# Unsummed weights for the sample's cached values: two key chunks on the column halves of TensorE, row blocks added afterwards

## The reference, cut to what matters

```
s = einsum('bqhcd,bkhcd->bhcqk', q, k) * (DIFF_HD ** -0.5)   # c: the two softmaxes
p = softmax(s, axis=-1)
a = p[:, :, 0] - lam * p[:, :, 1]
return einsum('bhqk,bkhe->bqhe', a, v)                       # v: 512 cached rows + 32 new ones
```

## Time and profile before

| | |
|---|---|
| median of 3 runs | 2252.79 us (2252.65 to 2253.14) |
| the profiled execution | 2255.4 us, its span 2253.5 us |
| PE busy | 2216.9 us, 98% of the span |
| DVE busy | 1196.4 us, 53% |
| ACT busy | 973.8 us, 43% |
| POOL busy | 856.4 us, 38% |
| mean granted clock of TensorE | 0.997 |

### The profile page before, as it was taken

The page is one execution under the profiler, slowest core; times in us unless marked ns, Lnnn a source line. Parts: engine busy times, 40 slices in busy tenths (PEclk is TensorE's granted clock), DMA queues, the critical chain, the costliest instruction groups (busy, mean ns, idle before and its releaser), DMA issues.

```text
span 2253.5 us, 43144 instructions
## 1 busy us (share of the span) xinstructions
PE 2216.9 (98%) x17640; PEld 2091.3 (93%) x17640; DVE 1196.4 (53%) x2018; ACT 973.8 (43%) x1876; POOL 856.4 (38%) x378
## 2 busy tenths in 40 slices
PE   6999999999999999999999999999999999999998
PEld 6889888889999999999988889888899999999998
DVE  5676665545456563256255666644463556523553
ACT  5555554344323453244345555533352334523443
POOL 4244223234343433443443343232243434434433
PEclk9999999999999999999999999999999999999999
DMA  4232222222222222322322232222222222223222
GB/s 164 68 109 76 91 68 94 73 82 80 75 76 94 76 88 79 107 82 71 103 89 72 86 104 81 75 82 73 82 78 78 76 94 81 77 86 105 94 65 98
DMA packets 81651, 193.69 MB, mean 86 GB/s; under 512 B 7504, under 2 KB 36528, under 8 KB 81456
## 3 DMA queue, kind: packets, MB, share of 16 engines
q1 hardware_dynamic: 59696, 173.50, 23.3%
q10 hardware_dynamic: 21760, 17.45, 2.4%
HBM read 177.50 MB, written 13.42 MB: 85 GB/s over the span
## 4 chain that ended last, share of the span: by engine, by line
PE 95%; ACT 2%; DVE 2%; issue 1%; POOL 0%; DMA 0%; ACTq 0%; DVEq 0%; POOLq 0%
PE ps L619 14%; PE ps L621 14%; PE ps L620 14%; PE ps L670 7%; PE ps L671 6%; PE ps L672 6%; PE ps L1023 4%; PE ps L1024 4%; PE ps L1022 4%; PE ps L693 2%; PE ps L771 2%; PE ps L803 2%; PE ps L838 2%; PE ps L649 2%; PE ps L896 2%; PE ps L763 1%
## 5 line engine op out<-in xcount | busy, mean ns | idle before, releaser
L497 POOL TENSOR_TENSOR wlo<-raw,whi 128x1024 fp32r<-128x1024 f32 (+1 forms) x330 | 768.0, 2347 | 1056.4 <-ACT whi L1081 1056.4
L619 PE MATMUL ps<-hl,whi 128*128 128x272 f32 x2432 | 704.0, 289 | 0.0
L621 PE MATMUL ps<-hl,wlo 128*128 128x272 f32 x2432 | 701.2, 288 | 0.0
L620 PE MATMUL ps<-hl,whi 128*128 128x272 f32 x2432 | 700.0, 288 | 0.0
L619 PEld LDWEIGHTS ps<-hl,whi 128*128 128x128 f32 x2432 | 458.6, 189 | 1.5
L621 PEld LDWEIGHTS ps<-hl,wlo 128*128 128x128 f32 x2432 | 457.6, 188 | 0.0
L620 PEld LDWEIGHTS ps<-hl,whi 128*128 128x128 f32 x2432 | 457.0, 188 | 0.0
L1081 ACT ACTIVATE whi<-raw 128x1024 fp32r<-128x1024 f32 (+1 forms) x330 | 313.4, 998 | 203.0 <-PE ps L1024 176.6
L670 PE MATMUL ps<-whi,hl 128*128 128x256 f32 x1216 | 353.1, 290 | 4.6 <-ACT rawk L1176 4.3
L671 PE MATMUL ps<-wlo,hl 128*128 128x256 f32 x1216 | 344.6, 283 | 0.0
L672 PE MATMUL ps<-whi,hl 128*128 128x256 f32 x1216 | 344.1, 283 | 0.0
(11 more groups left out here) (223 smaller groups left out, 3286.1 us busy)
## 6 DMA issues: line engine op xcount, KB each, us to landing
raw<-in_w_units_dram SPq DMA_DIRECT2D x260, 512.0 KB, 4.6
raw<-in_w_down_units_dram SPq DMA_DIRECT2D x64, 352.0 KB, 3.4
out_new_k_prompt_dram<-rawk ACTq DMA_DIRECT2D x8, 512.0 KB, 3.0
out_new_v_prompt_dram<-vd ACTq DMA_DIRECT2D x8, 512.0 KB, 3.0
raw<-in_w_first_dram SPq DMA_DIRECT2D x6, 512.0 KB, 5.0
out_y_dram<-x SPq DMA_DIRECT2D x8, 272.0 KB, 6.1
kc_n<-in_cache_k_dram SPq DMA_DIRECT2D x8, 256.0 KB, 2.9
vc_n<-in_cache_v_dram SPq DMA_DIRECT2D x8, 256.0 KB, 3.5
```

The source lines that it names most:

```text
L497: e.tensor_tensor(wlo[:, s, a:b], raw[:, s, a:b], whi[:, s, a:b].bitcast(F32), ALU.subtract).then_inc(*S.up("w_ready", ("lo", j, part)))
L619: e.matmul(out, wh, hi, start=(c == 0), stop=False)
L620: e.matmul(out, wh, lo, start=False, stop=False)
L621: ins = e.matmul(out, wl, hi, start=False, stop=(c == KC - 1))
```

## The change

In the sample's steps, ACT copies all 64 columns of each chunk into `aTs`. `aTt` and `weights_of_sample` go. PE multiplies all 64 columns with the chunk's values. Even chunks go to PSUM partitions 0 to 63, odd ones to 64 to 127, in the same bank. Four row blocks of 32 partial results then stand in the bank. ACT copies block 1 into `osum` (which lies in `rt`, free at that time), and DVE adds blocks 2, 3 and 0 to it one after another in `sum_of_sample`, the last into `odif`. For step 4 this stands after `combine(6)`, for step 9 at the end of the body. The last addition counts `dve_free_o` up.

```
-            aTs = sb("aTs", [P, TILES, DEC], F32, s)
-            aTt = sb("aTt", [P, TILES, DEC], F32, s)
+            aTs = sb("aTs", [P, TILES, 2 * DEC], F32, s)
...
+        osum = rt[0:DEC, 0, 0:HW]
...
-                            acquire("t", act=2, dve=2)
+                            acquire("t", act=2)
...
-                        acquire("o", act=1)
+                        acquire("o", act=1, dve=int(ib == NT))
+                        e.wait_ge(*S.at("act_free_t", ("aT", n)))
...
-                            e.wait_ge(*S.at("dve_free_t", ("aT", n)))
...
-                                ins = e.matmul(pv("o", DEC, HW), aTs[0:r, c, :], v, start=(c == 0), stop=(c == NT))
+                                rows = slice(2 * DEC * (c % 2), 2 * DEC * (c % 2 + 1))
+                                ins = e.matmul(ps[rows, BANK["o"]:BANK["o"] + HW], aTs[0:r, c, :], v, start=(c < 2), stop=(c >= NT - 1))
...
-                            e.activation(aTt[:, 0:NT, :], v[:, 0:NT, DEC:2 * DEC], ACT.Copy).then_inc(*S.up("act_free_t"))
-                            e.activation(aTt[0:DEC, NT, :], v[0:DEC, NT, DEC:2 * DEC], ACT.Copy).then_inc(
-                                *S.up("act_free_t", ("aTt", n)))
+                            e.activation(aTs[:, 0:NT, :], v[:, 0:NT, :], ACT.Copy).then_inc(*S.up("act_free_t"))
+                            e.activation(aTs[0:DEC, NT, :], v[0:DEC, NT, :], ACT.Copy).then_inc(
+                                *S.up("act_free_t", ("aT", n)))
...
+                            e.activation(osum, ps[DEC:2 * DEC, BANK["o"]:BANK["o"] + HW], ACT.Copy).then_inc(*S.up("act_free_o", key=("o", n)))
...
+                    def sum_of_sample(n):
+                        hh = steps[n][0]
+                        e.wait_ge(*S.at("act_free_o", ("o", n)))
+                        for g in (2, 3, 0):
+                            e.wait_ge(*S.own())
+                            ins = e.tensor_tensor(osum if g else odif[0:DEC, NT, ds(p * 2 * HW + hh * HW, HW)],
+                                                  ps[g * DEC:(g + 1) * DEC, BANK["o"]:BANK["o"] + HW], osum, ALU.add)
+                            ins.then_inc(*(S.up("dve_step") if g else S.up("dve_free_o", ("osum", n))))
...
                     for n in range(10):
                         combine(n)
+                        if n == NT + 2:
+                            sum_of_sample(NT)
                         if n + 2 < 10:
                             maxes(n + 2)
-                        weights_of_sample(n)
...
+                    sum_of_sample(9)
```

More of the change, by code:

```diff
@@ L830, in values @@
                         hh, ib = steps[n]
-                        acquire("o", act=1)
+                        acquire("o", act=1, dve=int(ib == NT))
+                        e.wait_ge(*S.at("act_free_t", ("aT", n)))
                         if ib < NT:
-                            e.wait_ge(*S.at("act_free_t", ("aT", n)))
                             if n == 0:
@@ L1266, in out @@
                         e.wait_ge(*S.own())
-                        dst = odif[0:r, ib, ds(p * 2 * HW + hh * HW, HW)]
-                        e.activation(dst, pv("o", r, HW), ACT.Copy, scale=rinv[0:r, n % 4, 0:1] if ib < NT else 1.0).then_inc(
-                            *S.up("act_free_o", key=("o", n)))
+                        if ib < NT:
+                            e.activation(odif[0:r, ib, ds(p * 2 * HW + hh * HW, HW)], pv("o", r, HW), ACT.Copy, scale=rinv[0:r, n % 4, 0:1]).then_inc(
+                                *S.up("act_free_o", key=("o", n)))
+                        else:
+                            e.activation(osum, ps[DEC:2 * DEC, BANK["o"]:BANK["o"] + HW], ACT.Copy).then_inc(*S.up("act_free_o", key=("o", n)))
                     take_filled(-1)
```

## The result

The changed kernel takes 2261.14 us (median of 7 runs, 2260.3 to 2262.57), the kernel before 2253.14 in the same comparison (7 runs, 2252.16 to 2257.37). The ratio is 1.0034, its 95% interval 1.0025 to 1.0044. So the change makes this kernel slower by 8 us, and the time lies above the predicted range of 2245.5 to 2258.5. The profiled execution took 2261.51 us.

A forecast was written before the change was run, and what follows sets the result against it. PE, 95% of the chain and busy 98% of the span, was taken as the bound. From the median 2252.8 us, 6.9 saved on PE and 2.1 lost to waits gave 2248.0, with an 8-in-10 range of 2245.5 to 2258.5.

The forecast's parts named there:

- The saving on PE: In the sample's matmuls eight passes become four rounds: 0.43 us a step, 6.9 us over 16 steps.
- The round of 0.11: From L649's four quarters abreast on PE: a round of 128 columns takes 0.11 us however many stand side by side.
- The hidden sum at step 4: DVE's three additions after step 4, 0.95 us, end before the maxima can start, with 0.2 us of cover.
- The wait that is added: After step 9 ACT's square waits for DVE's sum, 0.74 us later; PE loses 0.35 at the queries six times, 2.1 us.
- the list: ACT's square has 14 waits, DVE's two last; it starts 0.10 us after them, or later if they are passed first.
- the forecast: The likeliest outcome: PE's saving less the added wait at the queries gives 2248.0 us; chance 0.42.
- its rival: POOL gets in ahead of DVE's last rotation of the keys; 8.3 us more, 2256.3 us; chance 0.30.
- the blocked case: At the keys DVE's L1724, blocked by POOL's half, ends at about 223.05, so PE's transposes and scores wait; chance 0.30.
- the same 0.10 and 0.03: At the queries, 0.10 us from L1724's end to PE's transposes, and 0.03 lost as the first weight load isn't made ahead.
- The two waits: With DVE blocked, PE waits at the keys' transposes (0.54 and 0.03) and scores (0.79 and 0.03), 1.4 us a body.

The follow-up runs named there:

- e7: Changed kernel with the change in step 4 of each body alone, step 9 summing its weights as before; 2251.56 us, ratio 0.9986 to the kernel before.
- e6: Kernel before plus two additions of 32x144 on DVE at the end of each body; 2264.53 us, ratio 1.0046.
- e3: Kernel before plus three additions of 32x128 into scratch at the end of each body, matmuls unchanged; 2266.48 us, ratio 1.0054.
- e5: Changed kernel with a one-element memset (0.1 us) on POOL ahead of its first half of lo D 3; 2248.97 us, ratio 0.9980 to the kernel before.

## Why the prediction was wrong

- **The saving on PE**: right in kind, 0.376 instead of 0.43 a step, 6.0 instead of 6.9 us. The round of 0.11 that was taken from L649 holds; what was left out is the later second pass behind a change of shape with 64 columns. The rule cited from the Trainium skill, "TensorE: Matmul & The Clock Gate", section "The mechanism", that loads overlap matmuls only where the row group differs, is not what these halves show: they share all rows, and eight passes start in 0.59 instead of 1.02. The prediction took from it that the saving would be nought; the rule speaks of loads alone, and does not say that by itself.
- **The hidden sum at step 4**: right (e7).
- **The wait that is added**: right. The square came 0.70 later against 0.74 predicted, PE lost 0.34 a body against 0.35, in the six bodies named. The three additions took 0.92 (185.48 to 186.40) against 0.95, where 3 times 0.29 and 2 times 0.03 would have been 0.93. The square begins 0.08 after the last of them, against 0.10, so most of the list seems to be passed before they end.
- **The choice between the forecast and its rival**: this is the step that failed. I worked out that L1724 would begin at 220.47 and POOL at 220.46, called it undecided, and gave the blocked case 0.30 where the sum itself put POOL ahead. In the trace POOL was 0.013 to 0.016 ahead in all six bodies. The margin was right to the hundredth. That alone would be partly luck, since the rows of one body are rounded to 0.01. But the trace before has six such bodies: L1724 on the keys begins 0.361 to 0.377 ahead of POOL there, and the queries' L1724 ends 0.507 to 0.523 ahead of the transposes. With the same 0.10 and 0.03, POOL comes out 0.01 to 0.02 ahead in each of the six, so the sign could be read. The mistake was to take 0.01 for too little to tell, and then to let it favour the order of before. Since DVE's delay and POOL's start both hang on PE there, the margin is nearly the same in all bodies, and its sign decides for all six at once. The same bodies in e6, which has no wait to tie DVE to PE, do fall on both sides.
- **The price of the rival**: 1.4 a body predicted, 1.91 measured. The two waits were put at 0.57 (keys) and 0.82 (scores); they are 1.40 and 0.5. I let the keys' transposes wait for L1724 alone. They also need a PSUM bank that holds the queries, and DVE frees that bank with L1739 (L1737 before), which stands behind the last rotation on DVE: it begins at 219.88, takes 0.75 for one, and PE begins at 220.72. The row had both lines; I read L1737 only as work that delays the scores. So the rival's time of 2256.3 should have been 2252.8 - 6.0 + 2.1 + 11.5 = 2260.4 with the median then known, and the upper end of the range, 2258.5, was too low with it.
- **The clock**: left out of the sum. The windows of the changed kernel at the third key wait of the first layer (start and end, length, PE, PEld, DVE, ACT and POOL busy with counts, granted clock, DMA share, GB/s):

```profile
294.00:298.00 4.00, 2.76 (x20) 2.11 (x19) 3.63 (x5) 1.19 (x4) 3.51 (x2) 1.00 0.01 2
298.50:301.50 3.00, 3.00 (x19) 2.75 (x20) 1.44 (x4) 0.08 (x1) 0.00 (x0) 0.50 0.00 0
302.00:305.00 3.00, 3.00 (x24) 2.48 (x24) 1.84 (x7) 1.83 (x8) 0.00 (x0) 1.00 0.54 186
```

  PE had stood still for 1.23 us ahead of the keys' transposes at 296.25, and for 3.4 us from 298.35 the granted clock was 0.50, which is 1.2 GHz. It happens again at 1264.3, and not behind the other four key waits. From the first key transpose to the end of the first scores these two bodies take 1.57 us more than before, the other four 0.51. So the two falls cost 1.06 us each there, 2.1 us of this execution, in places where the kernel before has no such stretch. e6 has one behind one of its four long key waits (152.3), e3 none behind its six, and the kernels whose keys don't wait have none there. So such a wait can be followed by a fall of the clock, and need not be. Elsewhere both kernels have such stretches too, and they differ: 42.4 and 1172.2 in this one, 6.8 us each; 58.8 (6.8 us) and 1175.0 (3.4 us) before. The terms hold none of this, so that the medians agree with them to 0.4 us is closer than they can promise.

## What to carry to other kernels

Before adding work behind a hand-over, follow the delayed chain to every point where it meets an operation of another engine that shares a resource with it, and write down the order of the two starts and its margin. Where the sum says that the order turns, by however little, price the turned order as the likely case, and price it by all that stands behind the blocked operation, bank releases too. When the turned order is the trouble, it can be cheaper to take the consumer's wait away where it isn't needed (13.6 us here) or to hold the other engine for 0.1 us (12 us) than to give the change up.

## What the runs showed of the hardware

- **DVE's rotation and POOL's `lo`, both with two inputs in SBUF, exclude each other for the whole instruction, and a hundredth of a microsecond decides.** POOL ahead by 0.005 to 0.017: DVE's 0.33 becomes 2.55 to 2.57. DVE ahead by 0.003 to 0.033: DVE keeps 0.33, and POOL's 2.39 becomes 2.55 to 2.58. The Trainium skill, "SBUF — State Buffer", section "Who interferes with whom", has the rule: a DVE operation with two SBUF inputs and a GpSimd operation that reads SBUF contend, the first to start has the ports for its whole length, and the other is blocked. These runs agree, and POOL's memset in e5, which reads nothing, ran beside DVE's L1729 (217.36 to 217.46, and L1729 from 217.39) without lengthening it.
- **Column halves run abreast**: four rounds of two passes, 0.109 us a round for 128 columns (0.16 for the first) and 0.007 between the two of a round.
- **The first pass behind a change of shape costs more with wider weights**: the second starts after 0.16 us with 64 stationary columns, after 0.13 with 32. "TensorEngine Tiling (Array Packing)", section "Key Properties", in the Trainium skill says that a change of mode drains the array; the gap of 0.21 ahead of L847 instead of 0.12 between equal matmuls, in both kernels, agrees with it and gives it a size here of 0.09 us.
